# The last layer norm of a decoder step, taken apart: gain ahead of the statistics, shift by two-row products, half of the tokens on TensorE and ScalarE

## The reference

```python
def layer_norm(x, g, b):
    mu = jnp.mean(xf, axis=-1, keepdims=True)
    var = jnp.mean(jnp.square(xf - mu), axis=-1, keepdims=True)
    y = (xf - mu) * lax.rsqrt(var + LN_EPS)
    return (y * g + b).astype(x.dtype)

def moe_ffn(x, ...):        # top-1 group of experts, then top-2 experts in it
    for e in range(N_EXPERTS):
        h = jax.nn.silu(xt @ w_gate[e]) * (xt @ w_up[e])
        y = y + combine[:, e:e + 1] * (h @ w_down[e]).astype(f32)

x = layer_norm(ALPHA * x + moe_ffn(x, ...), ln2_g, ln2_b)
```

## Time and profile before

| | |
|---|---|
| median of 3 runs | 1690.29 us (1689.28 to 1691.51) |
| profiled execution, its own time | 1685.43 us |
| its span, first to last instruction | 1683.7 us |
| TensorE matmul busy | 1590.7 us (94%) |
| VectorE busy | 687.0 us (41%) |
| ScalarE busy | 387.0 us (23%) |
| DMA over the span | 545.86 MB, mean 324 GB/s |
| granted TensorE clock, mean | 0.995 of full |

### The profile page before, as it was taken

The page is one execution under the profiler, slowest core; times in us unless marked ns, Lnnn a source line. Parts: engine busy times, 40 slices in busy tenths (PEclk is TensorE's granted clock), DMA queues, the critical chain, the costliest instruction groups (busy, mean ns, idle before and its releaser), DMA issues.

```text
span 1683.7 us, 23718 instructions
## 1 busy us (share of the span) xinstructions
PE 1590.7 (94%) x10374; PEld 1070.4 (64%) x10374; DVE 687.0 (41%) x991; ACT 387.0 (23%) x398; POOL 43.6 (3%) x79
## 2 busy tenths in 40 slices
PE   8999999999999999999999988998898899889985
PEld 8999999999999999983533523434234234225322
DVE  6547678648585575554511110121021111103606
ACT  6444555523354332330000000000000000000000
POOL 2000000012000000000000000000000000000000
PEclk9999999999999999999999999999999999999998
DMA  8675465579656759979999999999999999999996
GB/s 254 187 213 164 137 189 162 151 203 329 195 162 179 232 180 306 285 284 385 429 428 427 427 428 429 429 429 428 428 429 429 429 428 429 428 429 428 428 415 216
DMA packets 252719, 545.86 MB, mean 324 GB/s; under 512 B 6080, under 2 KB 219152, under 8 KB 228320
## 3 DMA queue, kind: packets, MB, share of 16 engines
q1 hardware_dynamic: 245888, 527.06, 82.9%
q0 software_dynamic: 4640, 15.47, 2.9%
q10 hardware_dynamic: 2112, 2.16, 0.4%
HBM read 537.73 MB, written 6.95 MB: 323 GB/s over the span
## 4 chain that ended last, share of the span: by engine, by line
PE 74%; DMA 22%; DVE 2%; issue 0%; ACT 0%; DVEq 0%; ACTq 0%
PE bank L608 12%; PE bank L609 12%; PE bank L961 12%; PE bank L610 12%; DMA ring_low<-wu 10%; PE bank L893 10%; DMA ring_high<-wu 9%; PE bank L867 5%; PE bank L1015 3%; PE bank L651 2%; DMA ring_high<-wd 1%; DMA ring_low<-w_in 1%; DMA reg_uv<-x_t 1%; PE bank L979 0%; PE bank L1009 0%
## 5 line engine op out<-in xcount | busy, mean ns | idle before, releaser
L610 PE MATMUL bank<-x_hi,w_lo 128*128 128x264 f32 x1216 | 344.3, 283 | 0.0
L608 PE MATMUL bank<-x_hi,w_hi 128*128 128x264 f32 x1200 | 343.4, 286 | 0.1
L609 PE MATMUL bank<-x_lo,w_hi 128*128 128x264 f32 x1200 | 340.0, 283 | 0.0
L1236 DVE TENSOR_TENSOR w_lo<-ring_low,w_hi 128x2048 fp32r<-128x2048 f32 x107 | 244.8, 2289 | 153.1 <-ACT w_hi L1068 152.6
L893 PE MATMUL bank<-ring_low,reg_pk 128*64 128x512 f32 x1008 | 225.4, 595 | 34.7 <-DMA ring_low<-wu 28.5
L893 PE MATMUL bank<-ring_high,reg_pk 128*64 128x512 f32 x1024 | 228.2, 595 | 26.0 <-DMA ring_high<-wu 26.0
L1068 ACT CAST w_hi<-ring_low 128x2048 fp32r<-128x2048 f32 x107 | 203.6, 1903 | 138.5 <-PE bank L610 87.2
L610 PEld LDWEIGHTS bank<-x_hi,w_lo 128*128 128x128 f32 x1216 | 228.0, 187 | 0.0
L608 PEld LDWEIGHTS bank<-x_hi,w_hi 128*128 128x128 f32 x1200 | 226.1, 188 | 1.2 <-issue 0.8
L609 PEld LDWEIGHTS bank<-x_lo,w_hi 128*128 128x128 f32 x1200 | 226.2, 189 | 0.1
L893 PEld LDWEIGHTS bank<-ring_low,reg_pk 128*64 128x64 f32 x1008 | 69.4, 137 | 186.3 <-issue 125.7
(11 more groups left out here) (337 smaller groups left out, 1727.8 us busy)
## 6 DMA issues: line engine op xcount, KB each, us to landing
ring_low<-w_in SPq DMA_DIRECT2D x76, 1024.0 KB, 5.8
ring_high<-wg SPq DMA_DIRECT2D x34, 2048.0 KB, 35.3
ring_low<-wu SPq DMA_DIRECT2D x33, 2048.0 KB, 27.9
ring_high<-wd SPq DMA_DIRECT2D x32, 2048.0 KB, 33.2
ring_low<-wd SPq DMA_DIRECT2D x31, 2048.0 KB, 31.3
ring_low<-wg SPq DMA_DIRECT2D x30, 2048.0 KB, 35.3
ring_high<-wu SPq DMA_DIRECT2D x30, 2048.0 KB, 26.8
ring_low<-wo SPq DMA_DIRECT2D x16, 1024.0 KB, 6.7
```

The source lines that it names most:

```text
L608: pe.matmul(out, hi[k], of_hi[:, k, :], start=(k == 0), stop=False)
L609: pe.matmul(out, hi[k], of_lo[:, k, :], start=False, stop=False)
L610: mm = pe.matmul(out, lo[k], of_hi[:, k, :], start=False, stop=(k == kk - 1))
L1236: dve.tensor_tensor(lo_of(q), raw_of(q), hi_of(q).bitcast(F32), ALU.subtract).then_inc(lo_ready, 1)
```

## The change

Six things change together, all of them from the last pair of experts on.

1. The norm of tile tt is written as gain * x * r + (gain * (-mean * r) + bias), with r the reciprocal deviation. `gain_part` makes gain * x (`scaled_acc`) ahead of the statistics' end, three of four quarters between the scatters' adds, the fourth quarter later. The broadcasts of gain and bias are gone. The gain in all partitions comes from four two-row products (`gain_out`) and four copies on ScalarE; the parameters are loaded as eight rows by GpSimd, behind the hidden product of the last pair's first expert.
2. The second summand is a product of two rows: (-mean * r, 1) for the tokens, with (gain, bias) for the columns. VectorE makes -mean * r, eight small products turn it into rows, ScalarE copies them, and `shifted` multiplies, into PSUM.
3. Tile 0 is finished by VectorE, one pass per quarter (`scaled`). Tile 1 is finished by TensorE, which adds `spread` (a diagonal matrix of r) times `scaled_acc` to the same bank, and ScalarE copies it out.
4. A quarter's scatter on TensorE stands inside the next quarter, behind its fourth of eight blocks.
5. The stores of the two tiles are interleaved, the sample rows in the middle; TensorE reads `plan` ahead of the last pair.
6. VectorE aggregates right behind the last statistics, ahead of the samples' add and the branch.

```diff
+        ln2_gain = low[:, 1, 0:D]
+        scaled_acc = low[:, 2, :].rearrange("p (a c) -> p a c", c=D)
+        ln2_rows = reg_pk[:, KD * P:KD * P + 512]
...
-            for a, par in enumerate((ln2g, ln2b)):
-                sp.dma_start(ln2p[:, a, :], par.partition_broadcast(P)).then_inc(ln2_in, 16)
...
+            store(0, 0)
+            store(0, 1)
+            store(1, 0)
+            store(1, 1)
+            sp.wait_ge(ys_ready, 1)
+            for nn in range(4):
+                sp.dma_start(y[2 * P:2 * P + NS, 512 * nn:512 * nn + 512], acc_s[32 * nn:32 * nn + NS, :]).then_inc(y_out, 16)
+            store(1, 2)
+            store(0, 2)
+            store(1, 3)
+            store(0, 3)
...
+            pool.wait_ge(hid_ready, 2 * NPAIR - 1)
+            for c in range(4):
+                for a, par in enumerate((ln2g, ln2b)):
+                    pool.dma_start(ln2_rows[32 * c + a:32 * c + a + 1, :], par[512 * c:512 * c + 512].unsqueeze(0)).then_inc(rows_in, 16)
...
+            def gain_out():
+
+                for c in range(4):
+                    rows = slice(32 * c, 32 * c + 2)
+                    mm = pe.matmul(psum[c if c < 2 else 4 + c][:, :], ident[rows, 32 * c:32 * c + 1].broadcast_to([2, P]), ln2_rows[rows, :], start=True, stop=True)
+                return mm
+
             def down_last(i):
 
+                pe.wait_ge(rows_in, 16 * 8)
+                pe.wait_ge(pick_ev, i + 1)
+                gain_out().then_inc(gain_mm, 1)
                 hid_transposed(i, 1)
...
+                        if c and k == 3:
+                            scatter_last(i, c - 1)
                     mm.then_inc(w_used, 1)
-                    if c:
-                        scatter_last(i, c - 1)
...
+            def last_norm(made):
+
+                pe.wait_ge(shift_ready, 1)
+                for tt in range(2):
+                    for c in range(4):
+                        mm = pe.matmul(psum[0][32 * c:32 * c + 2, P * tt:P * tt + P], stat[:, tt, 4, 0:2], ident[:, :], start=True, stop=True)
+                mm.then_inc(shift_mm, 1)
+                pe.wait_ge(shift_ev, 1)
+                for c in range(4):
+                    shifted(0, c, psum[c])
+                for c in range(3):
+                    shifted(1, c, psum[5 + c])
+                pe.wait_ge(quarter_ready, 1)
+                sample_average(0)
+                pe.wait_ge(spread_ready, 1)
+                for c in range(4):
+                    bank = psum[5 + c] if c < 3 else psum[0]
+                    if c == 1:
+                        pe.wait_ge(y_ready, 1)
+                        shifted(1, 3, psum[0])
+                        sample_average(1)
+                    if c == 3:
+                        pe.wait_ge(xg_ready, made + 1)
+                    pe.matmul(bank[:, :], spread, scaled_acc[:, 1, 512 * c:512 * c + 512], start=False, stop=True).then_inc(y_acc, 1)
...
+            act.wait_ge(shift_mm, 1)
+            act.copy(shift_rows[0:98, :], psum[0][0:98, 0:2 * P]).then_inc(shift_ev, 1)
+            act.activation(spread, ident[:, :], ACT.Identity, scale=mv[:, 1, 3:4]).then_inc(spread_ready, 1)
+            for c in range(4):
+                act.wait_ge(y_acc, c + 1)
+                act.copy(acc[:, 1, 512 * c:512 * c + 512], psum[5 + c if c < 3 else 0][:, :]).then_inc(ya_ready, 1)
+                if c == 0:
+                    act.wait_ge(l_var, 4)
+                    act.activation(mv[:, 2, 2:3], mv[:, 2, 1:2], ACT.Sqrt, bias=eps).then_inc(l_std, 1)
...
+            def gain_part(tt, c):
+
+                cols = slice(512 * c, 512 * c + 512)
+                dve.tensor_tensor(scaled_acc[:, tt, cols], acc[:, tt, cols], ln2_gain[:, cols], ALU.mult).then_inc(xg_ready, 1)
...
-            def centred(n):
...
-                dve.scalar_tensor_tensor(out=acc[:, tt, cols], in0=acc[:, tt, cols], scalar=mv[:, tt, 0:1], in1=ln2p[:, 0, cols],
-                                         op0=ALU.subtract, op1=ALU.mult).then_inc(y_mul, 1)
...
-                dve.wait_ge(y_mul, n + 1)
-                dve.scalar_tensor_tensor(out=acc[:, tt, cols], in0=acc[:, tt, cols], scalar=mv[:, tt, 3:4], in1=ln2p[:, 1, cols],
+                dve.wait_ge(rank_two, c + 1)
+                dve.scalar_tensor_tensor(out=acc[:, 0, cols], in0=scaled_acc[:, 0, cols], scalar=mv[:, 0, 3:4], in1=psum[c][:, :],
                                          op0=ALU.mult, op1=ALU.add).then_inc(y_ready, 1)
```

116 lines of the change are left out of this document (66 added, 50 removed).

## The result

The changed kernel took 1695.92 us (median of 7 runs, 1692.62 to 1696.49) against 1690.36 of the kernel before on the same chip (7 runs, 1687.49 to 1691.67): ratio 1.0028, 95% interval 1.0019 to 1.0037. The forecast was 1689.1 and the range ended at 1693.8. By this ratio the change made the kernel some 4.7 us slower; the two medians are 5.6 apart.

The account below looks back on a forecast made before the run. Bound: the last quarter, scatter and adds, then VectorE's sixteen passes. Engines end 3.2 us earlier, bunched stores give part back: 1682.45 against 1683.7, -1.2, so 1690.3 becomes 1689.1 us; range 1687.0 to 1693.8.

Parts of the forecast that it names:

- Clock: Last norm on TensorE: the sum assumed full clock for the products behind the shift, with no loss.
- rival B: Products behind the shift run at half clock, TensorE becomes the bound: +3.3 us, or +1 midway; chance 0.28.
- Both signs that were named for being wrong: Last norm: granted clock 0.5 during the two-row products; VectorE waiting over 1 us for the first sample average.
- The two broadcasts of 1 MB: Queue behind the last weights: dropping the gain and bias broadcasts frees nothing that waits, 0.
- Quarters: Last down projection: last adds start 0.6 us later, aggregation follows at once; reciprocal 0, bounds -0.5 and +0.6.
- Gain products: Ahead of the first quarter: four two-row products run side by side in a 1.42 us TensorE gap, cost 0.
- rival C: Row groups on TensorE run one after the other: +5.2 us, 1695.5; chance 0.10.
- Chain to the first result: Reciprocal to VectorE's first result: shift, transposes, copy and first two-row product cost 1.0 us, up to 2.3.
- The rest: Remaining norm: fewer VectorE passes, engines end 3.2 us earlier; sample rows ready at 1676.2, stores give part back.
- rival A: Final stores not bunched, end follows VectorE's last result: -3.2 us at most, half of it taken, 1688.0; chance 0.17.
- Stores: Kernel end: four 256 KB stores issued behind the sample rows, 0.34 us apart, fill the DMA for 2.8 us.

Follow-up runs that it names:

- warm_thin: The changed kernel with 14 idle products of two rows and 128 columns on TensorE before the shift; ratio to the kernel before 1.0030.
- warm: The changed kernel with 14 idle full-array products of 128 columns on TensorE before the shift; 1692.31 us, ratio to the kernel before 1.0004.
- no_bcast: The kernel before without its two 1 MB broadcasts of gain and bias; one execution, tail 51.72 us against 50.54.
- late: The changed kernel with the eight small sample-row broadcasts issued only when the last weight unit has landed; 1694.33 us, ratio to the kernel before 1.0025.
- warm_late: The changed kernel with the edits of both warm and late; 1689.85 us, ratio to the kernel before 0.9997.
- held: warm_late with two more idle products behind the first four two-row products and two ahead of the eighth; ratio to the kernel before 1.0011.
- best_b: best_a with four more idle full products, two behind the first four two-row products and two ahead of the eighth; ratio to the kernel before 1.0000.
- gain_late: The changed kernel with the third quarter's two gain passes and one of the fourth's moved into VectorE's wait; ratio to the kernel before 1.0018.
- behind: warm_late with each scatter behind the next quarter again and VectorE's copies ahead of the adds; ratio to the kernel before 1.0013.
- best_a: The changed kernel with 12 idle products, late small broadcasts, earlier sample averages and root, and later third-quarter gain passes; ratio to the kernel before 1.0009.
- best_c: best_b with the stores in the order in which the pieces are ready; ratio to the kernel before 1.0008.
- before_warm: The kernel before with 14 idle full products behind its sample products; one execution, tail 52.54 us against 50.54.

## Why the prediction was wrong, by its steps

- **Clock, the step that failed first.** The forecast took full clock behind the shift and gave rival B 0.28. The argument against B was that the gap between the last dense products and the shift is shorter than before. The gap was as short as said (3.36 us of idle, before 3.81), and didn't save the clock; `warm_thin` filled it completely and lost it all the same. What the argument had to ask was what kind of products fill it and follow: B's own "what follows are thin bursts". Both signs that were named for being wrong came, 0.50 under the two-row products and 1.56 us of waiting for the first sample average. B was priced at +3.3; `warm` against the change gives 3.3 in the tail, 4.1 in the ratios. That the numbers agree is partly luck, for `warm` still has half clock under its last diagonals; but single terms fit too: transposes and first product +1.2 (4.65 against 3.44 below), predicted +1.3, the seven two-row products +1.8 (3.79 against 1.99), predicted +1.7. The Trainium skill, TensorE: Matmul & The Clock Gate, section Why this matters for your kernels, warned of half clock behind an idle gap. The trace agrees: half clock stood behind the gap of 3.36 us. The runs add that a gap filled with two-row products did the same as an idle one.
- **The two broadcasts of 1 MB, the second step that failed.** The prediction put this at 0: dropping them "frees nothing that waits, since they stand behind those weights in the same queue". They did stand behind them, but something else moved up in their place, eight broadcasts of 512 columns to 32 partitions each, and with these as direct followers the last of the 16 parts of the unit lands 22.8 to 23.5 after its issue instead of 22.15 (23.50 in the change). `no_bcast` shows it in the old kernel, `late` and `warm_late` its removal. Price 1.2 us at the fourth quarter (23.63 against 22.40); against no follower at all 2.1 at the landing, 1.6 at the fourth quarter. No rival had it.
- **Quarters: right in mechanism and nearly in size.** From the start of quarter four to the last adds: 8.16 us after (1662.33 to 1670.49), before 7.43 (1655.55 to 1662.98). The prediction had +0.6, measured +0.7. The aggregation follows at once and the reciprocal comes 4.04 behind the last adds (1674.53), before 4.70: it won back 0.66 where I had 0.6. So the reciprocal is late by little more than the landing.
- **Gain products: right.** 1.14 us for four, the first quarter at its old place; rival C is refuted (row groups run side by side, one after the other would be 3.4). The 1.14 is read with the pipeline's tail, as is the 1.12 of one two-row product alone (`held`): four take as long as one, and seven take 1.99 (`warm_late`), which is two rounds of 0.86 and 0.27. By the factor of 3.07 in the Trainium skill (TensorE: Matmul & The Clock Gate, Part 3) I had estimated 1.12 for a round without its tail; the trace doesn't bear it out, the 0.86 of the sum was right. ScalarE's copies ended as said: the table load behind them comes 8.39 after the issue (1647.09), predicted 8.7 (1641.9 - 1633.16), and the root is done before the first quarter's result.
- **Chain to the first result.** Predicted +1.0. At full clock (`warm_late`) 3.44 from reciprocal to VectorE's end of the first pass (1673.18 to 1676.62), before 2.44 (1667.68 to 1670.12): +1.0. The terms fit one by one: from the first transpose to the copy 0.68 (1673.61 to 1674.29), predicted 0.42 + 0.27, the copy 0.37 for 0.4, from the first two-row product to VectorE 1.16 (1674.71 to 1675.87) as said. At half clock it was 4.65.
- **The rest: a size that was off.** I had the first result 1.0 later, but took the sample rows' moment, 1676.2, over from before as it was. Their chain starts behind the first result in both kernels and is as long in the new one (6.18 in `warm_late`, 6.56 in `held`, 6.05 before), so they are late by that 1.0 too. VectorE has fewer passes in this stretch now, but 1.48 of the 6.18 are waits for the two averages on TensorE (0.51 and 0.97), where it had none before. With the term mended the sum at full clock is -0.2 instead of -1.2; measured -0.3 (`warm_late`) and +0.6 (`held`), and counted from the start of the fourth quarter, which came at different moments, +0.1 and +0.3. VectorE's own end came as summed: 44.66 in `warm_late`, predicted 44.4 (1677.6 - 1633.16). The forecast's gain was never there in this order, and rival A, which needed the sample rows 1 us earlier, still less. `best_b`, where they come earlier, has 49.32.
- **Stores: right in sum.** They are bunched behind the sample rows, 1.39 for these four, and from the issue of the sample rows to the end it is 6.39, predicted 6.26. The last four are issued 0.41 to 0.49 apart, not 0.34, and the DMA was full for 2.5 us behind them (1690.5 to 1693), predicted 2.8:

```profile
1690.50:1691.00 0.50, 0.00 (x0) 0.00 (x0) 0.00 (x0) 0.00 (x0) 0.00 (x0) 1.00 1.04 385
...
1692.50:1693.00 0.50, 0.00 (x0) 0.00 (x0) 0.00 (x0) 0.00 (x0) 0.00 (x0) 0.50 1.05 348
1693.00:1693.50 0.50, 0.00 (x0) 0.00 (x0) 0.00 (x0) 0.00 (x0) 0.00 (x0) 0.50 0.37 135
```

The sum of what was measured: landing +1.2, quarters +0.1 (0.7 less 0.66), first pass at half clock +2.2 (4.65 less 2.44), makes +3.5 at VectorE's first result; from there to the end it is 1694.4 - 1679.18 = 15.2 in the change, before 1683.7 - 1670.12 = 13.6: +1.6. Together 5.1 of the 5.2. Both failed steps are on this path, and each alone would have used up the 1.2 us that I had forecast. Against the forecast, whose tail was 49.3, the change's 55.7 is 6.4 more: 3.3 is what `warm` gives back, 2.1 what taking the followers away gives back behind it, and 1.0 is between `warm_late` and the forecast, the size of the term of the sample rows.

## What to carry to other kernels

Work moved onto TensorE near the end of a kernel should be priced at half clock too, unless dense products run right beside it; two-row products were cheap here only at full clock, and didn't keep it themselves. When a transfer is taken out of a queue, ask what becomes the neighbour of the transfer that everybody waits for, even if all of this stands behind it. And a moment taken over from the old profile ("when they are ready, at 1676.2") has to be followed through the new order like any other, if only one of its steps moves.

## What the runs showed of the hardware that was not expected

- Thin products and the clock: above, 3.39 us of two-row products against 3.39 us of full ones in the same place, ratio 1.0030 against 1.0004. In the changed kernel the clock came back only during the last diagonals (full 128-row products): full again from 50.10 after the issue, 1688.8, where the first of the last three had started at 1684.93.
- A dip in most executions with the gain products: in seven of the eleven kernels that have them, one execution each (warm, late, gain_late, behind, best_a, held, best_c), the clock was half for 3.4 us from 6.3 to 7.1 after the issue on, while the first quarter began, and the fourth started some 0.65 late where its weights were there (22.66 to 22.74 in five runs, against 22.00 and 22.01 in the two without the dip). It is absent in the change, warm_late, warm_thin and best_b, and in the three kernels without gain products. What decides it is open.
- The 16 parts of the last 2 MB unit land over 3.4 (best_a) to 6.6 us (before_warm); the last of the 16 is what releases TensorE.
- A branch on TensorE that jumps over the code of the further pairs took 3.77 us in the kernel before, 3.50 in `no_bcast` and 3.95 in `before_warm`. In the change the norm stands first in the branch: entering it took 0.07 (1668.71), and the jump over the rest came behind the norm's products in the program (3.34 at 1681.94) and held nothing up. Only in `before_warm` was the jump on the path.
- Four products of 32-bit floats with K=2 and 512 columns on four row groups take 1.14 us at full clock, one alone 1.12; eight of 128 columns and M=2 on four column groups 0.62.
